# Expert weights in two-chunk transfers, and a recurrent stage with its split steps and squared decay elsewhere

## The reference, cut to what matters

```python
h = silu(x_e @ w_gate[e]) * (x_e @ w_up[e]);  y_e = h @ w_down[e]
```

```python
r = sigmoid(u @ w_a + b_a);  i_g = sigmoid(u @ w_x + b_x)          # u: 256 x 1408, after a convolution
log_a = -8 * softplus(-lam) * r;   a = exp(log_a)
b = sqrt(-expm1(2 * log_a)) * (i_g * u)
hs[t] = a[t] * hs[t-1] + b[t];     y = (hs * gelu(gate)) @ w_out   # 1408 x 1024
```

## Time and profile before

| | us |
|---|---|
| median of 3 runs | 1810.52 |
| lowest, highest | 1806.41, 1811.04 |
| the profiled execution | 1809.85 |
| its span, first to last instruction | 1807.8 |
| PE, DVE, ACT, POOL busy in it | 1523.9, 787.8, 579.6, 33.8 |

### The profile page before, as it was taken

The page is one execution under the profiler, slowest core; times in us unless marked ns, Lnnn a source line. Parts: engine busy times, 40 slices in busy tenths (PEclk is TensorE's granted clock), DMA queues, the critical chain, the costliest instruction groups (busy, mean ns, idle before and its releaser), DMA issues.

```text
span 1807.8 us, 27194 instructions
## 1 busy us (share of the span) xinstructions
PE 1523.9 (84%) x11250; PEld 1156.5 (64%) x11250; DVE 787.8 (44%) x1166; ACT 579.6 (32%) x834; POOL 33.8 (2%) x39
## 2 busy tenths in 40 slices
PE   6999997799976676666666799888999989889999
PEld 3788874568842111121211688447999989779999
DVE  4352345466641101010101755545555475865653
ACT  4332034475321000000001531544333354743332
POOL 2000020000000000000000000000000000100000
PEclk8999998899967776676767897989999999889999
DMA  9655455543729999999999452952455534335540
GB/s 393 247 220 193 155 214 215 201 164 112 304 93 422 422 421 421 421 422 421 422 420 422 187 188 91 359 200 94 170 182 185 187 140 167 136 117 187 187 164 24
DMA packets 60573, 437.95 MB, mean 242 GB/s; under 512 B 6736, under 2 KB 6992, under 8 KB 7600
## 3 DMA queue, kind: packets, MB, share of 16 engines
q1 hardware_dynamic: 59616, 430.99, 61.3%
q0 software_dynamic: 560, 5.01, 0.7%
q10 hardware_dynamic: 288, 0.32, 0.1%
HBM read 435.25 MB, written 1.05 MB: 241 GB/s over the span
## 4 chain that ended last, share of the span: by engine, by line
PE 44%; DMA 21%; DVE 8%; ACT 3%; issue 2%; SPq 1%; PEld 0%; PEldq 0%; DVEq 0%; ACTq 0%
PE bank L653 41%; DMA ring<-in_w 21%; PE bank L989 2%; DVE ring_r L1609 1%; PE bank L657 1%; SPq L559 1%; DVE arena L1912 1%; ACT ring_r L1299 1%; DVE norm_t L1562 1%; PE bank L1015 0%; DVE arena L2034 0%; ACT arena L1453 0%; DVE arena L1870 0%; DVE H L1599 0%; DVE arena L2035 0%
## 5 line engine op out<-in xcount | busy, mean ns | idle before, releaser
L653 PE MATMUL bank<-H_r,ring_r 128*128 128x256 f32 x3488 | 510.6, 288 | 18.5 <-DVE H_r L1586 18.5
L653 PEld LDWEIGHTS bank<-H_r,ring_r 128*128 128x128 f32 x3488 | 465.4, 196 | 24.0 <-issue 22.6
L653 PE MATMUL bank<-arena_r,ring_r 128*128 128x256 f32 x2776 | 400.9, 288 | 30.4 <-DVE ring_r L1609 24.5
L1609 DVE TENSOR_TENSOR ring_r<-ring,ring_r 128x2048 fp32r<-128x2048 f32 x136 | 319.3, 2350 | 235.5 <-ACT ring_r L1299 235.2
L653 PEld LDWEIGHTS bank<-arena_r,ring_r 128*128 128x128 f32 x2776 | 371.9, 195 | 47.6 <-issue 23.2
L1299 ACT ACTIVATE ring_r<-ring 128x2048 fp32r<-128x2048 f32 x136 | 259.5, 1909 | 218.8 <-PE bank L653 174.9
L989 PE MATMUL bank<-ring,arena 128*32 128x512 f32 x1024 | 197.7, 866 | 108.4 <-DMA ring<-in_w 106.4
L989 PEld LDWEIGHTS bank<-ring,arena 128*32 128x32 f32 x1024 | 25.8, 126 | 265.2 <-DMA ring<-in_w 227.2
L1870 DVE TENSOR_TENSOR arena<-arena,bank 64x512 f32<-64x512 f32 x16 | 11.1, 692 | 289.0 <-ACT arena L1401 289.0
L1401 ACT ACTIVATE arena<-bank 64x512 f32<-64x512 f32 x16 | 9.4, 588 | 372.3 <-PE bank L989 372.3
L1015 PE MATMUL bank<-ring,arena 128*32 128x256 f32 x1024 | 85.7, 487 | 21.4 <-DMA ring<-in_w 13.6
(11 more groups left out here) (245 smaller groups left out, 1267.6 us busy)
## 6 DMA issues: line engine op xcount, KB each, us to landing
ring<-in_w SPq DMA_DIRECT2D x408, 1024.0 KB, 10.5
ring<-in_bias POOLq DMA_DIRECT2D x1, 2048.0 KB, 10.8
consts<-in_consts POOLq DMA_DIRECT2D x1, 1439.0 KB, 9.9
X<-in_x SPq DMA_DIRECT2D x1, 1024.0 KB, 5.3
arena<-in_ctx SPq DMA_DIRECT2D x1, 1024.0 KB, 7.8
arena<-in_decay POOLq DMA_DIRECT2D x1, 1024.0 KB, 11.7
out_t<-X SPq DMA_DIRECT2D x4, 256.0 KB, 2.0
wide<-in_wide POOLq DMA_DIRECT2D x1, 256.0 KB, 11.8
```

Source lines behind the costliest of these rows:

```text
L653: i = nc.tensor.matmul(o, lhsT, rhs, start=start, stop=stop, skip_group_check=grouped)
L1609: v.tensor_tensor(r(lo), lo, r(hi), ALU.subtract).then_inc(lo_ready, 1)
```

## The change

It has three parts.

1. The expert chunks are loaded two at a time, 2 MiB into two neighbouring slots with one semaphore increment; the host lays each pair out so that a partition's 16 KiB lie together. SyncE waits until both old chunks are used. TensorE waits for the pair.
2. ScalarE computes exp(2 log a) into `rnn_d` (now four tiles) ahead of exp(log a), with a scale column made once at the start; VectorE no longer multiplies a by a.
3. The VectorE part of the scan is a step of its own for each tile (`rnn_tile`), and four splits have fixed places: that of `rnn_out` 2 ahead of `rnn_gate` 1, of 3 ahead of `rnn_scan` 2, of 4 ahead of `rnn_tile` 10, of 5 ahead of `rnn_out` 3. In the list `rnn_out` 1 stands ahead of the last scan; on TensorE's own list nothing moves.

```diff
-        s += [("rnn_out", 0)] if g == len(RNN_GROUPS) - 1 else []
-        s.append(("rnn_scan", g))
-    s += [("rnn_out", j) for j in range(1, (RNN_T + 1) // 2)] + [("rnn_add",)]
+        s += [("rnn_out", 0), ("rnn_out", 1)] if g == len(RNN_GROUPS) - 1 else []
+        s += [("rnn_scan", g)] + [("rnn_tile", i) for i in tiles]
+    s += [("rnn_out", j) for j in range(2, (RNN_T + 1) // 2)] + [("rnn_add",)]
...
+SPLIT_AT = {("rnn_out", 2): ("rnn_gate", 1), ("rnn_out", 3): ("rnn_scan", 2), ("rnn_out", 4): ("rnn_tile", 10),
+            ("rnn_out", 5): ("rnn_out", 3)}
...
+        x = SPLIT_AT.get(u, x)
...
+            def load_pair(s, source):
+                sp_eng.dma_start(ring[:, s:s + 2, :].rearrange("p a b -> p (a b)"), source).then_inc(landed[s], 16)
...
+                with sp_eng.Fori(1, full) as r:
+                    for i in range(SLOTS // 2):
+
+                        sp_eng.wait_ge(chunk_used, r * SLOTS + (FIRST_EXPERT + 2 * i + 2 - SLOTS))
+                        load_pair(2 * i, source[r, i])
...
-            for s in range(6, SLOTS):
-                load(s, w[FIRST_EXPERT + s])
-            for s in RING_USE[1][1]:
-
-                sp_eng.wait_ge(chunk_used, RING[FIRST_EXPERT + s][2] + 1)
-                load(s, w[FIRST_EXPERT + s])
+            for s in range(6, SLOTS, 2):
+                load_pair(s, pair_of(FIRST_EXPERT + s))
+            for s in RING_USE[1][1][::2]:
+
+                for half in range(2):
+                    sp_eng.wait_ge(chunk_used, RING[FIRST_EXPERT + s + half][2] + 1)
+                load_pair(s, pair_of(FIRST_EXPERT + s))
...
-                        pe.wait_ge(landed[slot_of(c)], 16 * landed_count(c))
+                        pe.wait_ge(landed[landed_slot(c)], 16 * landed_count(c))
...
+                    f(rnn_d[:, n, :], rec[:, i, :], ACT.Exp, scale=sp[:, 5, 8 + i:9 + i])
                     f(rec[:, i, :], rec[:, i, :], ACT.Exp, scale=sp[:, 7, 8 + i:9 + i]).then_inc(rnn_tanh, 1)
...
+                link(v.tensor_scalar(sp[:, 5, :], sp[:, 6, :], -2.0, None, ALU.mult))
...
-                    link(v.tensor_tensor(rnn_d[:, i % 2, :], rec[:, i, :], rec[:, i, :], ALU.mult))
-                    v.scalar_tensor_tensor(thr[:, i, :], rnn_d[:, i % 2, :], 1.0, thr[:, i, :], ALU.add,
+                    v.scalar_tensor_tensor(thr[:, i, :], rnn_d[:, n, :], 1.0, thr[:, i, :], ALU.add,
                                            ALU.mult).then_inc(rnn_sqrt_in, 1)
...
+    for c in range(FIRST_EXPERT, FIRST_SECOND, 2):
+
+        w[c:c + 2] = w[c:c + 2].transpose(1, 0, 2).reshape(2, P, CHUNK).copy()
```

More of the change, by code:

```diff
@@ L213, in plan_ring @@
             s = slots[(c - first) % len(slots)]
-            fills[s] = fills.get(s, 0) + 1
-            places.append((s, fills[s], last.get(s)))
+            sem_slot = s
+            if FIRST_EXPERT <= c < FIRST_SECOND:
+                sem_slot = s - s % 2
+            if sem_slot == s:
+                fills[s] = fills.get(s, 0) + 1
+            places.append((s, fills[sem_slot], last.get(s), sem_slot))
             last[s] = c
@@ L228, in landed_count, with landed_slot @@
     return RING[c][1]
+def landed_slot(c):
+    return RING[c][3]
+SPLIT_AT = {("rnn_out", 2): ("rnn_gate", 1), ("rnn_out", 3): ("rnn_scan", 2), ("rnn_out", 4): ("rnn_tile", 10),
+            ("rnn_out", 5): ("rnn_out", 3)}
 def with_splits(steps):
@@ L467, in build @@
         rec, inp = room(8481, RNN_T, T), room(11297, RNN_T, T)
-        thr, rnn_d = room(2816, RNN_T, T), room(14113, 2, T)
+        thr, rnn_d = room(2816, RNN_T, T), room(14113, 4, T)
         bank = [ctx.enter_context(nc.psum_tensor(f"bank{i}", [P, 512], F32)) for i in range(8)]
@@ L559, in load, with pair_of, pair_rounds @@
                 sp_eng.dma_start(ring[:, s, :], source).then_inc(landed[s], 16)
+            def load_pair(s, source):
+                sp_eng.dma_start(ring[:, s:s + 2, :].rearrange("p a b -> p (a b)"), source).then_inc(landed[s], 16)
+            def pair_of(c):
+                return w[c:c + 2].rearrange("t p f -> (t p f)").rearrange("(q x) -> q x", q=P)
+            def pair_rounds():
+                full = EXPERTS * 12 // SLOTS
+                source = w[FIRST_EXPERT:FIRST_SECOND].rearrange("(r s t) p f -> r s (t p f)", s=SLOTS // 2, t=2)
+                source = source.rearrange("r s (q x) -> r s q x", q=P)
+                with sp_eng.Fori(1, full) as r:
+                    for i in range(SLOTS // 2):
+                        sp_eng.wait_ge(chunk_used, r * SLOTS + (FIRST_EXPERT + 2 * i + 2 - SLOTS))
+                        load_pair(2 * i, source[r, i])
             def rounds(stage):
@@ L588, in _ @@
             sp_eng.wait_ge(merged_ready, 4)
-            for s in range(6, SLOTS):
-                load(s, w[FIRST_EXPERT + s])
-            for s in RING_USE[1][1]:
-                sp_eng.wait_ge(chunk_used, RING[FIRST_EXPERT + s][2] + 1)
-                load(s, w[FIRST_EXPERT + s])
+            for s in range(6, SLOTS, 2):
[4 more added lines that the diff above has]
+                load_pair(s, pair_of(FIRST_EXPERT + s))
             sp_eng.wait_ge(chunk_used, FIRST_EXPERT)
-            for s in RING_USE[1][2]:
-                load(s, w[FIRST_EXPERT + s])
-            rounds(2)
+            load_pair(RING_USE[1][2][0], pair_of(FIRST_EXPERT + RING_USE[1][2][0]))
+            pair_rounds()
             for i, s in enumerate(RING_USE[3][1]):
@@ L1009, in step_experts @@
                         s = KT + c
-                        pe.wait_ge(landed[s], 16 * landed_count(FIRST_EXPERT + 12 * e + s))
+                        at = FIRST_EXPERT + 12 * e + s
+                        pe.wait_ge(landed[landed_slot(at)], 16 * landed_count(at))
                         ck = ring[:, s, :].rearrange("p (k n) -> p k n", k=2)
@@ L2018, in step_rnn_decay, with step_rnn_tile @@
             def step_rnn_decay(g):
-                for i in RNN_GROUPS[g]:
+                for n, i in enumerate(RNN_GROUPS[g]):
                     dve.wait_ge(rnn_tanh, i + 1)
-                    link(v.tensor_tensor(rnn_d[:, i % 2, :], rec[:, i, :], rec[:, i, :], ALU.mult))
-                    v.scalar_tensor_tensor(thr[:, i, :], rnn_d[:, i % 2, :], 1.0, thr[:, i, :], ALU.add,
+                    v.scalar_tensor_tensor(thr[:, i, :], rnn_d[:, n, :], 1.0, thr[:, i, :], ALU.add,
                                            ALU.mult).then_inc(rnn_sqrt_in, 1)
[L2026 to L2037, removed]
+            def step_rnn_tile(i):
+                dve.wait_ge(rnn_sqrt, i + 1)
+                dve.wait_ge(rnn_gated, i + 1)
+                link(v.tensor_tensor(inp[:, i, :], inp[:, i, :], thr[:, i, :], ALU.mult))
+                dve.wait_ge(job_done, JOBS[("rnn_gate", min(i + 1, RNN_T - 1))].no)
+                link(v.tensor_tensor_scan(u_c[:, i, :], rec[:, i, :], inp[:, i, :], 0.0, ALU.mult, ALU.add))
+                link(v.tensor_tensor(u_c[:, i, :], gelu_g[:, i, :], u_c[:, i, :], ALU.mult))
+                link(v.tensor_copy(r(gelu_g[:, i, :]), u_c[:, i, :]))
+                v.tensor_tensor(r(u_c[:, i, :]), u_c[:, i, :], r(gelu_g[:, i, :]), ALU.subtract).then_inc(rnn_ready, 1)
             def step_rnn_add():
@@ L2053, in _ @@
                      "nsa_o": step_nsa_o, "nsa_out": step_nsa_out, "ffn_in": step_ffn_in, "ffn_add": step_ffn_add,
-                     "rnn_in": step_rnn_in, "rnn_decay": step_rnn_decay, "rnn_scan": step_rnn_scan,
+                     "rnn_in": step_rnn_in, "rnn_decay": step_rnn_decay, "rnn_tile": step_rnn_tile,
                      "rnn_add": step_rnn_add}
```

## The result

The changed kernel takes 1796.49 us (median of six runs, 1792.98 to 1800.44) against 1810.78 us; the ratio is 0.9925 with an interval of 0.9909 to 0.9942. Forecast were 1796.0 us and 14.5 us less; it is 13.6 (10.5 to 16.5) less. The profiled execution took 1796.20 us, its span is 1794.1.

What follows compares the result with a forecast made beforehand. DMA bytes bound the expert stage; TensorE waiting on VectorE's splits held the recurrent stage. Experts -5.8 (-7 + 0.9 + 0.3) and recurrent -8.7 gave -14.5 us: 1810.5 to 1796.0 us, 8 in 10 from 1790 to 1805.

Steps and rivals of the forecast that it cites:

- The rate: Expert stage: 16 KiB rows speed up the 448 us DMA stream, saving 7 us, with ends 12 us and nothing.
- The upper end: Expert stream: a fixed part of about 17 ns a row, halved in number, would save 12 us.
- The forecast window: Sign in the expert stage: 560 to 980 us should move some 427 GB/s with half the packets.
- the first rival: Expert stream already at its ceiling, rows' fixed part overlapping between packets; stays 421 GB/s, total 1803.0 us; chance 0.20.
- The start: Expert stage: stream restarts after two chunks of matmuls release slots instead of one, with DMA idle; +0.9 us.
- The start near 538.6 us: Sign in the expert stage: the stream should start near 538.6 us.
- The end of the experts: Behind the last landing: two chunks' matmuls delay 1.1 to 2.1 us, mostly hidden by 1.9 us slack; +0.3 us.
- The recurrent stage: Replay of TensorE, ScalarE and VectorE queues: addition to X comes sooner as split waits shrink; -8.7 us.
- The unchanged stream: Rival in the expert stage: the stream stays at 421 GB/s, total 1803.0 us; chance 0.20.
- the full price: Rival in the expert stage: longer rows save the whole 12 us, total 1791.0 us; chance 0.15.
- The new order: Rival in the recurrent stage: ScalarE's lateness holds the gain to 4 us, total 1800.7 us; chance 0.10.
- Nothing slowed: Rival in the expert stage: long rows slow each other or the writes, total 1823.0 us; chance 0.05.

Runs made afterwards that it cites:

- x3: Changed kernel with 2 MiB transfers but 8 KiB rows in DRAM; 421 GB/s, 455.6 us from first expert matmul to the first matmul after the last expert landing.
- x7: Kernel before plus two-chunk expert transfers and only the `rnn_out` 2 split moved ahead of gate 1; recurrent stage 148.1 us to the next norm's reciprocal.
- y2: Changed kernel unaltered, run and profiled a second time beside the others on the same chip; ratio 0.9928 to the kernel before.
- x1: Two-chunk expert transfers alone, recurrent stage as in the kernel before; ratio 0.9991 to that kernel.
- y1: Second run, in eleven executions, of two-chunk expert transfers alone with the old recurrent stage; ratio 0.9982 to the kernel before.
- x2: Recurrent stage's changes alone, expert chunks loaded one at a time as before; ratio 0.9958 to the kernel before.
- x5: Changed kernel with VectorE's product a*a back, keeping two-chunk transfers and new split places; recurrent stage 141.7 us from reciprocal to reciprocal.
- y3: Second run of the recurrent stage's changes alone, expert chunks loaded one at a time; ratio 0.9949 to the kernel before.
- x6: Changed kernel with old split places and scan by groups, keeping two-chunk transfers and ScalarE's squared decay; recurrent stage 148.6 us to the next norm's reciprocal.
- x8: Changed kernel with group 0's product a*a back on VectorE; ratio 0.9938 to the kernel before.
- y4: Changed kernel with group 0's product on VectorE and single chunks for the experts' first pair after the pause and last pair; ratio 0.9922.

## Why the prediction was right, and where it was off

**The rate.** I took 7 us between 12 and nothing. It is 6.8 (S to L), with the rows the cause. The forecast window, 427 GB/s, moved 428. The upper end, 12 us from the earlier trace rows, rested on 17 ns a row, against 9 to 10 ns by the rates measured. Two things made it too high. Rows 4 and 5 were of packets that shared the engines with another queue: read in the same way, as packet time, the stream alone gives some 14 ns (315 ns for 8 KiB at 416 GB/s, 616 for 16 KiB at 425). And packet time is not elapsed time: its share fell from 101.1 to 100.4% with the longer rows. That fits an overlap of a part of that price, as the first rival suspected, but no run isolates it. The argument for a value in the middle was right in size, though "two row lengths agree" was no proof: both rows had the same fault. The 425 GB/s that the Trainium skill (DMA: Bandwidth & Descriptors, "Measured (HBM→SBUF, 128 partitions, SWDGE, issued from GpSimd)") has for 16 MB is no ceiling here, since 32 KiB rows moved 431. The Trainium skill's rule of 1 MiB or more in a transfer (the same page, "Rules for kernel authors") agrees with x3, where 2 MiB with 8 KiB rows moved no more than 1 MiB did; what was left to gain lay in the rows.

**The start**, +0.9 us. The first pair was issued 2.14 us after S (536.68 - 534.54), the first single 1.30 us after it before (536.07 - 534.77): +0.84. Up to L this doesn't show: x3 issues its first pair as late (2.14 us after S) and has the S to L of before. So the forecast for S to L was -7 + 0.9 = -6.1 us against -6.8 measured, and where the 0.8 us was made up is open. The start near 538.6 us that the prediction gave as a sign has no row behind it: the first pair was issued at 536.68.

**The end of the experts** is the term that failed: +0.3 us forecast. L to N is 2.8 to 3.8 us longer in seven of the eight traces with the changed kernel's expert stage, and 0.3 us shorter in the eighth, x7. Two things are in it.

*The slack was read on the wrong engine.* I set the delay of the combination against 1.9 us of room before ScalarE's squares. But VectorE's queue has two splits, 4.49 us together, directly behind the combination, and then the first operation of the norm, which had waited only 0.43 us (the first two rows are of the kernel before, the last two of the changed one, where the wait is gone):

```profile
998.12 4.49 DVE L1609 TENSOR_TENSOR ring_r<-ring,ring_r 128x2048 fp32r<-128x2048 f32 x2
1003.04 0.42 DVE L1560 TENSOR_SCALAR norm_t<-bank 128x256 f32<-128x256 f32 x1 [0.43 <-PE bank L653]
```

```profile
993.59 4.50 DVE L1640 TENSOR_TENSOR ring_r<-ring,ring_r 128x2048 fp32r<-128x2048 f32 x2
998.00 0.42 DVE L1591 TENSOR_SCALAR norm_t<-bank 128x256 f32<-128x256 f32 x1
```

So the slack was about 0.5 us and not 1.9. Counted from L, the combination ends 2.5 us later in the changed kernel and the norm's reciprocal 1.9; 3.1 and 2.6 in y2; 1.3 and 0.8 in x7. The squares on ScalarE, for which the term was forecast, end only 0.5 us later (the last one waits 0.32 us for VectorE, the row at 993.59 above), but they were not what the next step waited for.

*TensorE's clock.* Of the 2.5 us, 0.9 is the second chunk (1.93 us against 1.07). The rest is the 16 matmuls that scatter the last results: 5.41 us in the changed kernel, at a granted clock of 0.66 from 987 to 992 us, and 3.72 us before, at 1.00:

```profile
993.00:998.00 5.00, 3.72 (x16) 2.96 (x16) 3.65 (x9) 4.41 (x3) 0.00 (x0) 1.00 1.02 423
1140.00:1150.00 10.00, 7.44 (x62) 3.81 (x63) 4.60 (x12) 6.06 (x23) 0.00 (x0) 1.00 1.01 424
```

In the profile after, a stretch in the attention also ran at 0.66 (1140 to 1150 us), and from the second norm behind the experts to N it took 2.7 us more than before; in the second profile (y2) that part took 0.2 us more, but the last two chunks took 2.47 us instead of 1.93 and the 16 matmuls of the second norm 6.36 instead of 5.21 (6.12 before).

I replayed matmuls at the speed that they had in the profile of before. In a stage where TensorE idles and works by turns that is not given. But the loss doesn't simply follow the pairs. In x7, which up to here runs the same steps as x1 and y1, the scattering matmuls took 3.72 us at a granted clock of 1.00, and L to N was 264.6 us, as without pairs (a timeline row and a window):

```profile
984.48 3.72 PE L681 MATMUL bank<-arena 128*128 128x256 f32 x16 [1.97 <-DVE arena L1907]
```

```profile
984.00:989.00 5.00, 3.72 (x16) 2.96 (x16) 3.65 (x9) 4.54 (x6) 0.00 (x0) 1.00 1.01 421
```

So of eight traces with pairs seven lost 2.8 to 3.8 us here and one lost nothing, while the three without pairs agree to 0.1 us. With pairs the loss is common, but the steps alone don't fix it; what decides where the clock falls is not shown.

**The recurrent stage**, -8.7 us, was -9.0 from M to A. The waits came where the replay had them: 1.58 us at gate 8 (1.3), 0.83 before `rnn_out` 4 (0.9), tile 4 late. One gain more had no term in my sum: the 16 matmuls of the following norm took 5.38 us instead of 6.55, so the stage gave 10.2 us to the reciprocal. The matmuls are the same in every kernel and only their granted clock differs: 5.38 us in the seven traces of the changed kernel, x2 to x5 and y3, 6.46 to 6.55 in the three of the old stage, 5.22 in x6, 6.70 in x8, 6.67 in y4, 3.77 in x7 (the clock was 0.69 in the changed kernel, 0.56 before, 1.00 in x7). So this gain came back with the changed stage each time, but the replay, with its speeds from the profile of before, could not give it. Together: -6.8 + 3.7 - 10.3 and -0.2 before S make -13.6 us from trace to trace, where the sum had -14.5. So the closeness of the total, 0.9 us from trace to trace and 0.5 us in the median, is in part luck: the loss behind the experts was 3.4 us more than forecast, and the stream, the recurrent stage and the norm gave 0.7, 0.3 and 1.2 us more, with 0.2 us before S.

**The rivals.** The unchanged stream and the full price are refuted by the rate. The new order holds what it should. Nothing slowed in the expert stage. The share of the parts is now known: order 7.8 us, squared decay 1.2 us on top, pairs 3.6 to 4.0 from S to N (7.1 in x7).

## What to carry to other kernels

Replay the queues of all engines across a change of order: moving one cause of a wait, or taking 5 us of work off the engine that is waited for, gave nothing or about 1 us here until the next split behind the same scans was moved too. Do the same for slack: it is the smallest room on any queue that the next step needs, here 0.5 us on VectorE and not 1.9 on ScalarE. In this kernel's stream, which is bound by DMA, longer contiguous rows brought the gain and fewer transfers brought none. Behind a stage in which TensorE idles, leave room in the sum for its clock: in seven traces of eight some three of seven microseconds were lost there.

## What the runs showed of the hardware

One core's loads from DRAM, issued by SyncE, moved 421, 428 and 431 GB/s with rows of 8, 16 and 32 KiB a partition, and 421 with 8 KiB rows in transfers twice as large. From S to L three traces of the same stream agree to 0.2 us, and eight with pairs to 0.5 us. The spread of the totals lies elsewhere: S itself comes at 531.4 to 535.4 us in the fourteen traces, and 2.6 us apart in two of the same kernel (x1, y1); S to N of the eight with pairs is 713.3 to 717.7 us. The same 16 matmuls took 3.72 us at a granted clock of 1.00 and 5.41 us at 0.69, in x7 and x1, which run the same steps up to there.
